# Four heads' key scores held, 20 early expert units, and one-hot rows split between VectorE and ScalarE

## What is computed

```python
q = (xt @ w_query).reshape(n, 8, 2, 128)
s1 = einsum('nhd,kd->nhk', q[:, :, 0], sub_keys_1)     # key scores, 128 per half
s2 = einsum('nhd,kd->nhk', q[:, :, 1], sub_keys_2)
v1, i1 = top_k(s1, 16);  v2, i2 = top_k(s2, 16)
cand = v1[..., :, None] + v2[..., None, :]             # 256 candidates
sc, ci = top_k(cand, 16)
experts = e1 * 128 + e2                                # e1, e2: the picked keys of each half
gate = softmax(sc)
act = gelu(einsum('nhkd,nd->nhk', u_table[experts], xt))
out = einsum('nhk,nhkd->nd', gate * act, v_table[experts])
```

## Time and profile before

| what | value |
| --- | --- |
| time, median of three | 4622.53 us |
| profiled execution, its own time | 4623.17 us |
| its span, first to last instruction | 4621.4 us |
| TensorE (PE) busy | 4310.1 us, 93% |
| VectorE (DVE) busy | 2676.7 us, 58% |
| GpSimd (POOL) busy | 2581.3 us, 56% |
| ScalarE (ACT) busy | 1060.7 us, 23% |
| mean granted TensorE clock | 0.976 of full speed |
| DMA traffic | 1082.02 MB, mean 234 GB/s |

### The profile page before, as it was taken

How to read it: one execution, slowest core, us unless ns; L and a number is a source line. 1 busy time by engine, 2 the same in 40 slices (tenths; PEclk the granted TensorE clock), 3 DMA queues, 4 the chain that set the end, 5 groups by cost and what they waited for, 6 DMA issues and landing times.

```text
span 4621.4 us, 71896 instructions
## 1 busy us (share of the span) xinstructions
PE 4310.1 (93%) x26508; PEld 4132.5 (89%) x26508; DVE 2676.7 (58%) x4808; ACT 1060.7 (23%) x1861; POOL 2581.3 (56%) x1653
## 2 busy tenths in 40 slices
PE   8999999999989998985888999999999999999997
PEld 8999888888889997985878999999999999999996
DVE  1000233334432323899796777787777777787776
ACT  1000122222221101100223222322323223223223
POOL 4445332222235453443335777787877878778783
PEclk9999999999999999997999999999999999999998
DMA  5222322222233221111457999999999999999994
GB/s 197 102 98 98 119 103 109 100 92 74 78 135 123 101 96 66 55 65 57 155 157 274 377 391 389 394 405 411 397 384 380 391 385 405 392 403 403 392 418 195
DMA packets 268537, 1082.02 MB, mean 234 GB/s; under 512 B 24496, under 2 KB 89136, under 8 KB 185264
## 3 DMA queue, kind: packets, MB, share of 16 engines
q0 software_dynamic: 74736, 544.24, 28.8%
q1 hardware_dynamic: 87840, 388.01, 22.5%
q10 hardware_dynamic: 105888, 148.96, 9.6%
HBM read 1019.65 MB, written 66.85 MB: 235 GB/s over the span
## 4 chain that ended last, share of the span: by engine, by line
PE 59%; DVE 12%; POOL 11%; DMA 8%; issue 7%; ACT 1%; ACTq 1%; DVEq 0%; POOLq 0%
PE banks L461 29%; PE banks L703 11%; PE banks L639 10%; POOL w_lo L356 8%; DMA work<-in_u_rows,idx_all 3%; POOL work L384 2%; DMA work<-in_v_rows,idx_all 2%; PE banks L530 2%; PE banks L691 2%; PE banks L492 2%; DMA rows_own<-in_u_rows,idx_all 1%; PE banks L500 1%; POOL rows_own L384 1%; DVE work L1312 1%; DMA work<-out_p 1%
## 5 line engine op out<-in xcount | busy, mean ns | idle before, releaser
L356 POOL TENSOR_TENSOR w_lo<-w_raw,w_hi 128x1024 fp32r<-128x1024 f32 x480 | 1153.1, 2403 | 385.5 <-ACT w_hi L1024 374.8
L362 POOL TENSOR_SCALAR w_hi<-w_raw 128x2048 fp32r<-128x2048 f32 x130 | 252.5, 1942 | 1480.3 <-PE banks L461 1273.9
L461 PE MATMUL banks<-mv_hi,w_hi 128*128 128x256 f32 x3648 | 864.2, 318 | 62.3 <-DVE mv_lo L1146 37.4
L461 PE MATMUL banks<-mv_lo,w_hi 128*128 128x256 f32 x3648 | 837.2, 311 | 0.0
L461 PE MATMUL banks<-mv_hi,w_lo 128*128 128x256 f32 x3648 | 836.3, 310 | 0.0
L703 PE MATMUL banks<-mv_hi,w_hi 128*128 128x384 f32 x2048 | 696.9, 340 | 78.4 <-DVE work L1439 61.4
L461 PEld LDWEIGHTS banks<-mv_hi,w_hi 128*128 128x128 f32 x3648 | 652.7, 190 | 126.2 <-issue 102.5
L1024 ACT ACTIVATE w_hi<-w_raw 128x1024 fp32r<-128x1024 f32 x480 | 508.6, 1060 | 982.2 <-PE banks L703 647.9
L639 PE MATMUL banks<-mv_hi,w_hi 128*128 128x384 f32 x2048 | 696.4, 340 | 17.6 <-POOL w_lo L356 13.9
L703 PE MATMUL banks<-mv_lo,w_hi 128*128 128x384 f32 x2048 | 690.6, 337 | 0.0
L703 PE MATMUL banks<-mv_hi,w_lo 128*128 128x384 f32 x2048 | 690.6, 337 | 0.0
(11 more groups left out here) (155 smaller groups left out, 4784.6 us busy)
## 6 DMA issues: line engine op xcount, KB each, us to landing
w_raw<-in_wstream SPq DMA_DIRECT2D x480, 512.0 KB
w_raw<-in_wstream SPq DMA_DIRECT2D x130, 1024.0 KB, 4.8
gate_matrix<-work ACTq DMA_DIRECT2D x12, 2048.0 KB, 9.2
work<-gate_matrix ACTq DMA_DIRECT2D x32, 768.0 KB
out_p<-work ACTq DMA_DIRECT2D x34, 320.0 KB, 2.2
work<-out_p ACTq DMA_DIRECT2D x34, 320.0 KB, 3.4
gate_scratch<-work ACTq DMA_DIRECT2D x32, 320.0 KB, 2.2
work<-gate_scratch ACTq DMA_DIRECT2D x16, 640.0 KB, 3.9
```

The costliest lines, as they stand in the source:

```text
L356: pool.tensor_tensor(w_lo[s][:, part], raw[s][:, part], w_hi[s][:, part].bitcast(f32), ALU.subtract) \
L362: pool.tensor_scalar(w_hi[s][:, :], raw[s][:, :], 1.0, 0.0, ALU.mult, ALU.add).then_inc(hi_done, 1)
L461: last = pe.matmul(acc(dst, h), a[s][:, P * k:P * k + P], b[h][:, k, :], start=(k == k_first and n == 0), stop=(k == k_last and n == 2))
```

## The change

Four edits. (1) `sc_sb` becomes eight buffers instead of two (HELD = 4 heads of two halves each); the loops of ScalarE and VectorE over heads handle four heads a trip, and `topk_done` starts at 8 instead of 2. The new buffers lie in `rows_own` and `W2`. (2) EARLY goes from 4 to 5, so 20 units are early and the gather stage has 236 units, with five groups of 12 and 22 of eight; the deal of the 513 steps follows. (3) TAIL goes from 4 to 8 and TAIL_PICKS from 3 to 6: six early units before the picks, two after, 12 in the G loop as before. (4) VectorE makes the one-hot rows of a quad with two `tensor_tensor` compares over [128, 4, 128] with broadcast operands, `oh1` first (`oh_equal`), then `oh2` (`oh_ready`). ScalarE multiplies `oh1` by the gate, one `activation` with a per-partition scale for each token, in place, and raises `oh_gated`, which TensorE now waits for as well. In ScalarE's order the gates of quad q + 1 stand before the evacuation of quad q. The last trip of the loop is written out apart, since it has no next quad.

```diff
--- before.py
+++ after.py
@@ -26,9 +26,10 @@
 GROUPS = KEYS // EG
 GT = 32
 GBLK = N2 // GT
-TAIL = 4
-TAIL_PICKS = 3
-EARLY = 4
+TAIL = 8
+TAIL_PICKS = 6
+EARLY = 5
+HELD = 4
 N_EARLY = EG * EARLY
 PICKS = PH * TOPK
 ROWS = 4
@@ -205,7 +206,8 @@
 
 
         qe = [area(0, T), area(T, T)]
-        sc_sb = [area(1280, T), area(1920, T)]
+        sc_sb = ([area(1280, T), area(1920, T)] + [rows_own[:, T * n:T * n + T] for n in range(3)]
+                 + [W2[:, T * n:T * n + T] for n in range(5, 8)])
         sc2 = area(2560, T)
         cand, cand2 = area(3200, 1280), area(4480, 1280)
         val = area(5760, 160).rearrange("p (b s k) -> p b s k", b=NB, s=2)
@@ -281,6 +283,7 @@
         gexp_in, gexp_done, picks_done, picks_full, picks_taken = (
             sem(n) for n in ("gexp_in", "gexp_done", "picks_done", "picks_full", "picks_taken"))
 
+        oh_equal, oh_gated = sem("oh_equal"), sem("oh_gated")
         oh_ready, g_full, g_evac = sem("oh_ready"), sem("g_full"), sem("g_evac")
         act_stored = [sem(f"act_stored{s}") for s in range(2)]
         act_in = [sem(f"act_in{e}") for e in range(EG)]
@@ -685,6 +688,7 @@
                             pe.wait_ge(gelu_done, n - 1)
                         act_step(s, k % KT_N, s)
                     pe.wait_ge(oh_ready, 16 * i + q + 1)
+                    pe.wait_ge(oh_gated, 16 * i + q + 1)
                     pe.wait_ge(g_evac, 16 * i + q + 1)
                     for t in range(4):
                         n = 4 * (q % 2) + t
@@ -961,16 +965,16 @@
 
             act.wait_ge(mv_ready, 4 * KT_N)
             act.sem_inc(sc_taken, 2)
-            with act.Fori(0, N_QUERY // 2) as i:
-                for s in range(2):
-                    c = 2 * i + s
+            with act.Fori(0, N_QUERY // 2 // HELD) as i:
+                for n in range(2 * HELD):
+                    s, c = n % 2, 2 * HELD * i + n
                     act.wait_ge(unit_done, U_QUERY + c + 1)
                     evacuate(qe[s], s).then_inc(q_evac, 1)
                     act.wait_ge(sc_full, c + 1)
                     act.wait_ge(topk_done, c + 1)
                     four, one = sc_parts(s)
-                    act.activation(sc_sb[s][:, 0:512], four, ACT.Copy)
-                    act.activation(sc_sb[s][:, 512:T], one, ACT.Copy).then_inc(sc_taken, 1)
+                    act.activation(sc_sb[n][:, 0:512], four, ACT.Copy)
+                    act.activation(sc_sb[n][:, 512:T], one, ACT.Copy).then_inc(sc_taken, 1)
 
             def early_activation(n, s, trip):
                 act.wait_ge(unit_done, U_PEER + n + 1)
@@ -998,9 +1002,20 @@
 
 
             act.sem_inc(g_evac, 2)
-            with act.Fori(0, GBLK // 2) as i:
+
+            def gate_rows(i, q):
+
+                act.wait_ge(oh_equal, 16 * i + q + 1)
+                for t in range(4):
+                    row = oh1[:, 4 * (q % 2) + t, :]
+                    last = act.activation(row, row, ACT.Copy, scale=pick_t[0][:, ds(2 * GT * i + 4 * q + t, 1)])
+                last.then_inc(oh_gated, 1)
+
+            def gate_trip(i, final):
                 for q in range(2 * GT // 4):
                     w, qq = q // 8, q % 8
+                    if q < 2 * GT // 4 - 1 or not final:
+                        gate_rows(i, q + 1)
                     act.wait_ge(g_full, 16 * i + q + 3)
                     if qq == 0:
                         act.wait_ge(g_stored[w], 16 + 16 * i)
@@ -1013,6 +1028,10 @@
                     if q in (8, 15):
                         early_activation(TAIL + 2 * i + q // 15, q // 15, TAIL // 2 + i)
 
+            gate_rows(0, 0)
+            with act.Fori(0, GBLK // 2 - 1) as i:
+                gate_trip(i, False)
+            gate_trip(GBLK // 2 - 1, True)
 
             for w in range(2):
                 act.wait_ge(g_stored[w], 16 + 16 * (GBLK // 2))
@@ -1320,19 +1339,18 @@
                     last = dve.max_index(out_i(b)[:, 8:16], out_v(b)[:, 8:16], alt(b))
                 return last
 
-            dve.sem_inc(topk_done, 2)
+            dve.sem_inc(topk_done, 2 * HELD)
             cand4 = cand.rearrange("p (b i j) -> p b i j", b=NB, i=TOPK)
             eq3 = eq.rearrange("p (n k) -> p n k", k=TOPK)
             eq4 = eq.rearrange("p (b n k) -> p b n k", b=NB, n=TOPK)
             full = [P, NB, TOPK, TOPK]
-            with dve.Fori(0, N_QUERY // 2) as i:
-                own.enter(i, 6 + 1 + 3 + 1 + 2 + 6)
+            def top_picks(i, h):
                 for s in range(2):
                     dve.wait_ge(sc_taken, 2 * i + s + 3)
                     dve.sem_inc(dve_apart, 1)
-                    top16(KEYS, lambda b: sc_sb[s][:, P * b:P * b + P], lambda b: sc2[:, P * b:P * b + P],
+                    top16(KEYS, lambda b: sc_sb[2 * h + s][:, P * b:P * b + P], lambda b: sc2[:, P * b:P * b + P],
                           lambda b: val[:, b, s, :], lambda b: idx_u[:, b, s, :]).then_inc(topk_done, 1)
-                dve.wait_ge(topk_done, 2 * i + 4)
+                dve.wait_ge(topk_done, 2 * i + 2 + 2 * HELD)
                 dve.tensor_copy(idx_f, idx_u)
                 own.done(dve.tensor_tensor(cand4, val[:, :, 0, :].unsqueeze(3).to_broadcast(full),
                                            val[:, :, 1, :].unsqueeze(2).to_broadcast(full), ALU.add))
@@ -1357,7 +1375,12 @@
                     own.wait()
                     own.done(dve.tensor_reduce(pick_e[z][:, :, ds(TOPK * i, TOPK)], eq4, AX.X, ALU.add))
                     own.wait()
-                own.leave(N_QUERY // 2)
+
+            with dve.Fori(0, N_QUERY // 2 // HELD) as trip:
+                own.enter(trip, HELD * (6 + 1 + 3 + 1 + 2 + 6))
+                for h in range(HELD):
+                    top_picks(HELD * trip + h, h)
+                own.leave(N_QUERY // 2 // HELD)
 
 
             g3 = pick_g.rearrange("p b (h k) -> p (b h) k", k=TOPK)
@@ -1393,13 +1416,12 @@
             with dve.Fori(0, GBLK // 2) as i:
                 for q in range(2 * GT // 4):
                     dve.wait_ge(g_full, 16 * i + q + 1)
-                    for t in range(4):
-                        n = 4 * (q % 2) + t
-                        tok = ds(2 * GT * i + 4 * q + t, 1)
-                        dve.tensor_scalar(oh2[:, n, :], iota, pick_t[2][:, tok], None, ALU.is_equal)
-                        last = dve.tensor_scalar(oh1[:, n, :], iota, pick_t[1][:, tok], pick_t[0][:, tok],
-                                                 ALU.is_equal, ALU.mult)
-                    last.then_inc(oh_ready, 1)
+                    four = [P, 4, KEYS]
+                    at = slice(4 * (q % 2), 4 * (q % 2) + 4)
+                    keys = iota.unsqueeze(1).to_broadcast(four)
+                    one, two = (p[:, ds(2 * GT * i + 4 * q, 4)].unsqueeze(2).to_broadcast(four) for p in pick_t[1:])
+                    dve.tensor_tensor(oh1[:, at, :], keys, one, ALU.is_equal).then_inc(oh_equal, 1)
+                    dve.tensor_tensor(oh2[:, at, :], keys, two, ALU.is_equal).then_inc(oh_ready, 1)
 
 
             dve.wait_ge(g_full, 2 + N2 // 4)
```

## The result

The changed kernel took 4655.12 us (4647.66 to 4659.93, 4 runs) where the kernel before took 4624.12 (4618.06 to 4627.13, 4 runs): ratio 1.0063, 95% interval 1.0047 to 1.0079. It is slower by 0.63%, outside the range given. The profiled execution took 4647.66 us, 24.5 more than the one before; 6.5 of the 31.0 us between the medians lie in neither profile.

The account below looks back on a forecast made before the run. TensorE, the busiest engine, was taken to set the pace, with waits on VectorE. Picks +3.5, unit after them +8.3, G loop +6.8, gather stage -26.7 sum to -8.1 us: 4623.17 becomes 4615.1, range 4587 to 4640.

Parts of the forecast that it names:

- the gather stage, -26.7 us: Gather stage: four fewer units at TensorE's pace give -33.3 us, eight more three-step slots cost +6.6.
- My bound by bytes, -10.8: Gather stage: smallest gain, -10.8 us, if bytes alone set the pace (four units of 1.05 MB at 388 GB/s).
- the rival built on it: Gather stage: bytes bound it, -10.8 us instead of -26.7, so 4631 us in all; chance 0.20.
- The +6.6 for eight more slots of three steps: Gather stage: 56 three-step slots instead of 48, each costing VectorE 0.83 us over a unit's 8.33.
- The G loop, +6.8 us: Gate-matrix loop: 245.0 us against 238.2, from TensorE's work, 45.8 of stalls behind ScalarE's stores and 13.9 of slow starts.
- The rival in which the stall goes: G loop: gates' wait is absorbed, loop 217 us, total 4587; with a weaker form at 4601, chance 0.24 together.
- the one in which ScalarE is the bound: G loop: four gates don't overlap, a quad costs ScalarE 2.21 us, loop +27, total 4642; chance 0.16.
- The picks, +3.5 us: Before the G loop: three more GpSimd splits during VectorE's selection delay the picks by 3.5 us, range 0 to 6.
- The picks come no earlier: Pick stage: holding four heads' scores removes none of VectorE's top-16 work, so it brings no gain.
- 3.5 + 8.3 = 11.8: Before the G loop: later picks, +3.5 us, plus one added early unit after the picks that nothing hides, +8.3.
- The signs named in advance: If right: shorter wait before picks (15 to 25 us), one-hot waits once a block, VectorE 60 to 75% busy, slower GpSimd pieces.
- Two signs of being wrong: From a list: one-hot waits every quad, trip under 36 us, gather stage only 11 us shorter at same GB/s, earlier picks.

Follow-up runs that it names:

- e7: Kernel before (16 early units) with VectorE's gather steps on half the columns and only half rows gathered; 4520.30 us, one execution.
- e8: Kernel before with 20 early units, VectorE's gather steps on half the columns and only half rows gathered; 4512.47 us, one execution.
- e9: Kernel before with its 513 steps dealt over the first 233 gather slots instead of the first 237; 4636.23 us, ratio 1.0016.
- e10: Kernel before with 20 early units and an even room of 6.5 for every slot of the deal; 4623.52 us, ratio 0.9989.
- e13: Kernel before with 20 early units, old rooms in the 12-slot groups and 6.5 in the 8-slot groups; 4628.60 us, ratio 1.0002.
- e1: Kernel before with only TAIL = 8, TAIL_PICKS = 6 and EARLY = 5 (20 early units); 4653.11 us, ratio 1.0067.
- e4: Changed kernel with the G loop's stores issued by SyncE instead of ScalarE; 4625.96 us, ratio 1.0009.
- e3: Kernel before with only HELD = 4 (scores of four heads held); 4618.47 us, ratio 0.9991.

## Why the prediction was wrong

**The step that failed: the gather stage, -26.7 us.** It was +7.3, so this term missed by 34.0 us. (The loop missed by +7.0 and its start by -8.2; together these are the 32.6 us between -8.1 and +24.5.) I priced four units at TensorE's pace although the DMA engines were 98% busy, and took one undisturbed stretch at 408 GB/s as proof of room. e7 and e8 show that TensorE's pace holds only when the rows arrive in time. My bound by bytes, -10.8, was too hopeful as well, and so was the rival built on it: it counted the stage's bytes as if the rate would stay, and left out that four more early units are read back (16 loads of 192 KB instead of 12). The stage's bytes fell from 818.73 to 815.26 MB, which is 9 us, but its rate fell as well, from 388 to 385 GB/s. TensorE stood still 26.4 us more, and its slower work grew by 14.2. That the same rows fall on fewer slots is only a small part of this: e9 has that density too, and lost some 7 us. Most of it comes with the layout that 20 early units give the stage; part of that was won back by moving the three-step slots (e10, e13), and the cause of the rest is open.

**The +6.6 for eight more slots of three steps** was the wrong term for this. A denser deal with the same slots (e9: 55 three-step slots) costs about 7 us, but the pauses fall on L707, at the V phases, and the number of such slots doesn't decide: e13 has 57 of them, e1 56, and e13's stage is 24 us shorter. Where they stand is worth 22 to 30 us.

**The G loop, +6.8 us**, was +13.8, by the mechanism that I gave. The stalls behind ScalarE's queue are 44.5 us in 11 pieces (45.8 forecast), and four gates take the 1.28 us that I expected; e4 removes the stalls. That the sum fits so well is in part luck: the stalls are some 2.5 and 5.8 us in turn, where I had 3.3 and 5.2. I missed 4.7 us of waits for the one-hots (L1424), and the slow starts are 252.0 - 185.3 - 44.5 - 4.7 = 17.5 instead of 13.9. The rival in which the stall goes needed SyncE's stores; the one in which ScalarE is the bound did not come.

**The picks, +3.5 us.** "The picks come no earlier" was wrong for the held scores. Counted from the first key scores, since the stages ahead of them already differ by some us from run to run, the transposes start after 324.7 us in the kernel before, 317.6 with held scores (e3), 329.6 with six early units ahead of them instead of three (e1), and 322.8 with both (the changed kernel). The other kernels agree with these four to within 0.8 us. Holding gives 7.1 us, and three more splits cost about 5, where I had 3.5. VectorE had not been waiting for scores: from its first to its last top-16 instruction it executes 1042 instructions in both e3 and the kernel before, and is busy 270.6 us instead of 278.7. The same instructions are stretched less; why, no run shows. Sum: the loop starts 3.6 us later, where 3.5 + 8.3 = 11.8 was forecast; 2.3 of the difference arose before the query stage, and the unit after the picks cost 7.9 us.

**The signs named in advance.** The wait before the picks fell to 32.0 us, not to 15 to 25. In the loop VectorE is busy 68%, GpSimd's four pieces take 6.6 us, and the one-hot groups wait once a block, right after the small store, all as said. Two signs of being wrong came: the gather stage wasn't shorter, and the picks were earlier, though not because VectorE had been waiting for scores.

**What stays open.** With the better deal 20 early units still make the stage 13 us longer (2095.7 against 2082.3), where bytes alone would take 9 off. Each 8-slot group is 1.2 us longer. A group of eight slots has 52 of the deal's 1514 rooms, now of 1483, so it takes 18.0 of the 513 steps instead of 17.6; these 0.37 steps are 0.39 MB, 1.0 us at 393 GB/s. Why the 12-slot groups take 3.8 us longer was not shown. With the old deal the loss is larger: at the same density e9's groups take 106.3 and 70.1 us and e1's 109.4 and 71.4.

## What to carry to other kernels

Where a stage has two resources near their limit, price a removed piece of work by the one that the last wait ends on: here DMA at 98%, and a stretch that went well says little about the next. After shortening a stage into which other work is dealt, fit the layout of that work anew: here that was worth more than the four units could have given by their bytes. When an engine gets new work in the middle of a loop, look at what its queue issues besides; moving two stores to another engine's queue was worth 29 us here.

## What was not expected of the hardware

A pause costs more than its length: after 5.19 us TensorE's next matrix instructions took 0.53 us instead of 0.34, and over the gather stage of the changed kernel slower work added 41.3 us to 104.8 of standing still. A small store issued by ScalarE right behind the 2048 KB one held ScalarE, its compute instructions too, until 5.9 us after the big store's issue. The same unchanged loop took 235.7 us at a granted clock of 0.96 and 249.9 at 0.93, so one profile of it says little about a change of 10 us.
